# Mixer B's prompt attention with keys and values formed per head, mask and rotary rows in the contraction, and mixer A's units across both key groups

## The chip, the cores and the metric

The kernel runs on one core of one Trainium2 chip. The metric is the device time of one execution in microseconds, lower is better. All arithmetic is on 32-bit floats. The engines are TensorE (PE), which the profile splits into matmuls (PE) and weight loads (PEld), VectorE (DVE), ScalarE (ACT), GpSimd (POOL), and SyncE (SP), whose queue issues all DMAs here.

## The reference

Two layers of a streaming encoder run over 512 prompt tokens and, with the same weights, over 8 running streams of 16 new tokens each, so 640 tokens in all (T). Each layer has two attention mixers over one input projection, a gate, an output projection, and a gated feed-forward network. Mixer A is sliding-window attention (8 query heads in 2 key groups, head size 64). Mixer B is latent attention: keys and values are a shared latent of 128 numbers per token (ckv), and a rotary key of 32 numbers.

```python
    q = jnp.einsum('btr,rhe->bthe', _rms_norm(cq, q_norm), w_uq)      # 8 heads, 64 + 32 numbers
    q_rope = _rope(q[..., NOPE_DIM:], pos)
    q_lat = jnp.einsum('bthn,rhn->bthr', q[..., :NOPE_DIM], w_uk)
    ckv = _rms_norm(ckv, kv_norm)
    kr = _rope(kr, pos)
...
    s = (jnp.einsum('bqhr,bkr->bhqk', q_lat, ckv) + jnp.einsum('bqhe,bke->bhqk', q_rope, krope)).astype(f32) * MLA_SCALE
    if mask is not None:
        s = jnp.where(mask[None, None], s, -jnp.inf)
    p = jax.nn.softmax(s, axis=-1).astype(ckv.dtype)
    return jnp.einsum('bhqk,bkr->bqhr', p, ckv)
...
    y_b = jnp.einsum('bthr,rhv->bthv', o_lat, w_uv).reshape(B, T, HEADS_B * V_DIM)
    g = jax.nn.sigmoid(x @ w_gate + b_gate)
    h = g[..., :D_MODEL] * (y_a @ w_proj_a) + g[..., D_MODEL:] * (y_b @ w_proj_b)
    x = _layer_norm(ALPHA * x + h @ w_out, ln1_g, ln1_b)
```

The prompt's mask lets a query see all keys up to the end of its own chunk of 64 tokens. The score can be formed in two ways: the query is carried into the latent space (q_lat, 128 numbers) and meets ckv, or the latent is carried into each head's key space (64 numbers) and meets the query there. Likewise for the values and w_uv.

## The kernel before, in words

Features lie on partitions, tokens along the free axis. Weights come in slabs of 128 x 2048, through a ring of two buffers: SP loads w_raw, ACT rounds it to w_hi, POOL forms the rest w_lo, and PE multiplies three products of the high and low parts (`dense`). When POOL is done with a slab, its buffer is loaded anew (raw_free). The big products use a fast 32-bit form in one pass. The attention products are plain f32: one matmul in the program is two instructions in the trace, called passes here.

PE's work is a list of numbered jobs (J_ names), each written into one of four pairs of PSUM banks, with DVE or ACT emptying them; `start_job(n)` waits until job n-4 was emptied. A layer goes through these stages.

1. The input projection: cq, ckv, rotary key, the queries q_a of mixer A, k_t, v_t. Then NOPE and ROPE, the two parts of w_uq, then J_LAT (q_lat of each head, by `full` at L1244, from q_nope and a zero-padded w_uk called ukp), and J_TOK, transposes of v_t and ckv_t into tokens on partitions. DVE empties each: q_rs are copies of rotary queries of the streams (L940), v_tok, v_new, ckv_tok and ckv_new (L871) come last.
2. 40 attention units (UNITS). "Ap" is 128 prompt queries of mixer A (8 units, four heads of one key group each), "As" one stream of mixer A (8), "Bp" 128 prompt queries and two heads of mixer B (16), "Bs" one stream of mixer B (8). Bp and Bs units are mixed in the list. A Bp unit with block index i has (i+1) x 128 keys. A unit's steps are scores (PE), peaks (DVE), exps (ACT), normalise (DVE), turn (PE transposes the probabilities), a copy of one half on ACT and one on DVE, values (PE) and take_out (DVE). PE's order is written out by hand:

```python
                for u in range(NU):
                    turn(u)
                    gate_quarter(8 + 3 * u)
                    if u + 2 < NU:
                        scores(u + 2)
                    gate_quarter(9 + 3 * u)
                    values(u)
                    gate_quarter(10 + 3 * u)
```

A gate quarter is six matmuls of the gate's projection (L1438), so that PE has work while the other engines run a softmax. Four quarters fill one PSUM bank, which ACT copies to `logits` (take_gate, L696) before the next gate starts; SP stores the logits and loads the next gate slab, and also the cached rows of each Bs unit (load_cache).
3. J_UV: the latent outputs times w_uv (L1466 to L1468). ACT and DVE split y_a into ya_hi and ya_lo and the result into yb_hi and yb_lo, then PROJ multiplies them.
4. The output projection, norms, and the feed-forward network, which the change doesn't touch.

## Time and profile before

| | |
|---|---|
| median of 3 runs | 2150.72 us (2148.73 to 2151.97) |
| the profiled execution, its own time | 2150.01 us |
| its span, first to last instruction | 2148.2 us |
| mean granted TensorE clock | 0.973 of full |
| busy: PE, DVE, POOL, ACT | 94%, 46%, 31%, 31% of the span |
| issue to landing of a 1024 KB slab | 4.8 us |

A busy share says how much of the span an engine had work in flight. The granted clock is given as a share of 2.4 GHz; 0.5 is 1.2 GHz. A line such as L1438 is the line of the kernel before, the names behind it are the tile written and the tiles read.

### The profile page before, as it was taken

The numbers are of one execution on the slowest core, as the hardware profiler recorded it, in microseconds if no ns is written. First come the engines' busy times: TensorE is split into PE (matmuls) and PEld (weight loads), VectorE is DVE, ScalarE is ACT, GpSimd is POOL, SyncE is SP. The second block draws the span as 40 slices with busy tenths as digits, with TensorE's granted clock in tenths as the row PEclk, the third lists the DMA queues.
The fourth block names the chain that finished last, engine by engine and source line by source line (L and its number), as shares of the span: only waits on it lengthen the run. The fifth ranks groups of instructions, "written<-read, shape, count | busy, mean of one in ns | idle before, by whom it ended". The sixth has DMA issues, their size and how long they took to land.

```text
span 2148.2 us, 33773 instructions
## 1 busy us (share of the span) xinstructions
PE 2013.6 (94%) x12730; PEld 1856.9 (86%) x12730; DVE 984.2 (46%) x1437; ACT 656.7 (31%) x1303; POOL 675.3 (31%) x312
## 2 busy tenths in 40 slices
PE   6799999999899999999899899999998999999992
PEld 5786777789899999999899667777997999999992
DVE  3546433344765432443354753333476643234436
ACT  2213323242344311232231233223422542123222
POOL 2230111013823334333723111011262433343265
PEclk9899999999999999999999999999999999999996
DMA  5322121223112112211131212211421211222121
GB/s 143 115 97 78 50 97 61 74 82 128 59 54 83 68 70 83 82 62 62 69 136 55 95 58 78 78 57 50 157 79 40 91 66 60 81 95 78 49 72 70
DMA packets 49614, 169.86 MB, mean 79 GB/s; under 512 B 7128, under 2 KB 12024, under 8 KB 41272
## 3 DMA queue, kind: packets, MB, share of 16 engines
q1 hardware_dynamic: 49496, 168.28, 22.3%
q8 instruction: 76, 1.25, 0.2%
q14 instruction: 42, 0.34, 0.0%
HBM read 151.83 MB, written 18.26 MB: 79 GB/s over the span
## 4 chain that ended last, share of the span: by engine, by line
PE 74%; issue 13%; POOL 5%; DVE 5%; ACT 2%; DMA 1%; SPq 0%; POOLq 0%; DVEq 0%; ACTq 0%
PE ps L1236 50%; PE ps L1438 10%; POOL w_lo L546 4%; PE ps L1350 2%; PE ps L1347 2%; PE ps L1412 2%; PE ps L1370 1%; PE ps L1357 1%; PE ps L1244 1%; PE ps L1356 1%; POOL sum_sq L570 1%; ACT probs L663 1%; PE ps L1402 1%; PE ps L1416 1%; PE ps L1329 1%
## 5 line engine op out<-in xcount | busy, mean ns | idle before, releaser
L546 POOL TENSOR_TENSOR w_lo<-w_raw,w_hi 128x1024 fp32r<-128x1024 f32 (+3 forms) x252 | 577.1, 2299 | 1451.8 <-ACT w_hi L628 1440.9
L628 ACT ACTIVATE w_hi<-w_raw 128x1024 fp32r<-128x1024 f32 (+3 forms) x248 | 235.2, 968 | 486.2 <-PE ps L1236 466.7
L1236 PE MATMUL ps<-x_hi,w_hi 128*128 128x320 f32 x1504 | 345.7, 311 | 26.1 <-POOL w_lo L546 26.1
L1236 PE MATMUL ps<-x_lo,w_hi 128*128 128x320 f32 x1504 | 344.7, 310 | 0.0
L1236 PE MATMUL ps<-x_hi,w_lo 128*128 128x320 f32 x1504 | 344.2, 310 | 0.0
L1236 PEld LDWEIGHTS ps<-x_hi,w_hi 128*128 128x128 f32 x1504 | 253.0, 189 | 27.8 <-ACT w_hi L628 20.3
L1236 PEld LDWEIGHTS ps<-x_lo,w_hi 128*128 128x128 f32 x1504 | 253.2, 189 | 0.0
L1236 PEld LDWEIGHTS ps<-x_hi,w_lo 128*128 128x128 f32 x1504 | 253.2, 189 | 0.0
L1438 PE MATMUL ps<-x_hi,w_hi 128*128 128x320 f32 x512 | 184.9, 361 | 11.9 <-ACT logits L696 11.7
L1140 DVE TENSOR_SCALAR f_conv<-f_ext,vec 128x656 f32<-128x656 f32 x44 | 67.2, 1527 | 224.6 <-ACT tail L796 222.7
L1236 PE MATMUL ps<-hf_hi,w_hi 128*128 128x320 f32 x704 | 160.7, 309 | 0.0
L1236 PE MATMUL ps<-hf_lo,w_hi 128*128 128x320 f32 x704 | 160.4, 308 | 0.0
L1236 PE MATMUL ps<-hf_hi,w_lo 128*128 128x320 f32 x704 | 160.2, 308 | 0.0
L1438 PE MATMUL ps<-x_hi,w_lo 128*128 128x320 f32 x512 | 159.3, 311 | 0.0
L1438 PE MATMUL ps<-x_lo,w_hi 128*128 128x320 f32 x512 | 159.0, 311 | 0.0
L1438 PEld LDWEIGHTS ps<-x_hi,w_hi 128*128 128x128 f32 x512 | 97.2, 190 | 54.9 <-issue 36.5
L1236 PEld LDWEIGHTS ps<-hf_hi,w_hi 128*128 128x128 f32 x704 | 117.5, 188 | 0.3
L1236 PEld LDWEIGHTS ps<-hf_lo,w_hi 128*128 128x128 f32 x704 | 117.6, 188 | 0.0
L1236 PEld LDWEIGHTS ps<-hf_hi,w_lo 128*128 128x128 f32 x704 | 117.6, 188 | 0.0
L1155 DVE TENSOR_TENSOR hf_lo<-f_h,hf_hi 128x640 f32 x44 | 82.7, 1879 | 46.5 <-ACT hf_hi L804 46.5
L1263 PE MATMUL ps<-x_hi,w_hi 128*128 128x320 f32 x256 | 62.8, 329 | 38.5 <-DVE x_lo L1089 30.0
L1438 PEld LDWEIGHTS ps<-x_lo,w_hi 128*128 128x128 f32 x512 | 97.8, 191 | 0.7
(221 smaller groups left out, 3274.9 us busy)
## 6 DMA issues: line engine op xcount, KB each, us to landing
w_raw<-in_slabs SPq DMA_DIRECT2D x88, 1024.0 KB, 4.8
w_raw<-in_slabs SPq DMA_DIRECT2D x20, 768.0 KB, 4.2
gate_logits<-logits SPq DMA_DIRECT2D x32, 320.0 KB, 2.1
gates<-gate_logits SPq DMA_DIRECT2D x16, 640.0 KB, 6.1
w_raw<-in_slabs SPq DMA_DIRECT2D x16, 640.0 KB, 3.9
ckvc<-in_ckvc SPq DMA_DIRECT2D x16, 256.0 KB, 2.7
ckvc_t<-in_ckvc_t SPq DMA_DIRECT2D x16, 256.0 KB, 2.8
x_in<-in_x_t SPq DMA_DIRECT2D x4, 640.0 KB, 8.6
```

The lines of the kernel that those rows point to most:

```text
L546: pool.tensor_tensor(w_lo[:, s % 2, c], w_raw[:, s % 2, c], w_hi[:, s % 2, c].bitcast(F32), ALU.subtract).then_inc(wlo_ready, 1)
L570: pool.tensor_tensor(sum_sq[:], sq[:, 0, :] if k == 1 else sum_sq[:], sq[:, k % 2, :], ALU.add).then_inc(added_sq, 1)
L628: A(w_hi[:, s % 2, c], w_raw[:, s % 2, c], ACT.Copy).then_inc(whi_ready, 1)
L663: A(pr, pr, ACT.Exp, bias=st_nm[:, b, t:t + 1], accum_out=st_sum[:, b, t:t + 1])
L1140: link(TSC(f_conv[:, 0:NC_], f_ext[:, 2:EXT], w(2), vec[:, bass.ds(V_CB + j, 1)], ALU.mult, ALU.add))
L1155: TT(row(hf_lo, jj), f_h[:], row(hf_hi, jj).bitcast(F32), ALU.subtract).then_inc(fh_lo_ready, 1)
L1236: ins = MM(out_[:, a, :], w, x[:, t, a * HT:(a + 1) * HT], start=t == 0 and w is wh and x is hi, stop=t == tiles - 1 and w is wl)
L1263: ins = MM(out_[:, a, :], w, x[:, t, a * HT:(a + 1) * HT], start=t == 0 and w is wh and x is x_hi, stop=t == KD - 1 and w is wl)
L1347: MM(sc, q_lat[:, h, i * P:(i + 1) * P], ckv_t[:, 0:n], start=True, stop=False)
L1350: ins = MM(sc, q_r[hp, h // 4, i * P:(i + 1) * P], kr_r[hp, 0:n], start=False, stop=True)
L1412: ins = MM(o[:, 0:2 * P], ckv_tok[:, k, :], pt[:, k * 256:(k + 1) * 256], start=k == 0, stop=k == i)
L1438: ins = MM(ps[:, 7, 0:HT], w, x[:, t, a * HT:(a + 1) * HT], start=t == 0 and w is wh and x is x_hi, stop=t == KD - 1 and w is wl)
```

## The change

For the prompt's mixer B the latent is carried into each head's space once, before the units. `kb` holds for each head 64 key rows (w_uk times ckv, jobs J_KN, with w_uk turned by J_WUK first), 32 rotary key rows, and 4 mask rows; `qb` the same rows of the query. One contraction over 100 rows then gives the masked score. DMAs write the rotary rows and the mask rows. `v_b` holds values per head (jobs J_V), so a Bp unit's output is y_b itself and no longer the latent. J_LAT and J_UV remain for the streams alone. ckv_tok and the zero-padded ukp are gone. A Bp unit's values are now two column halves of 64 outputs, one for each head.

An Ap unit takes heads of both key groups, two of each, so that successive score matmuls use rows 0 to 63 and 64 to 127 in turn, and successive value matmuls write output partitions 0 to 63 and 64 to 127 in turn.

`logits` is half as large: each gate is stored by itself, and ACT waits for the store of the gate before the last. DVE waits for six of a layer's stores ahead of its first peaks, since tiles now share memory with what is stored.

```diff
-J_NOPE, J_ROPE, J_LAT, J_TOK = 13, 17, 21, 29
-J_UV = 33
-J_PROJ = J_UV + 4
+J_WUK, J_KN, J_NOPE, J_ROPE, J_LAT, J_V, J_TOK = 13, 14, 18, 22, 26, 27, 31
+J_UV = 34
+J_PROJ = J_UV + 1
...
@@ SyncE, before the layers and at a layer's start
+            sp.wait_ge(mask_made, 16)
+            sp.dma_start(bass.AP(mask_dram.tensor, 0, [[SEQ + P, NB], [1, CHUNK]]),
+                         inp["mask_q"][0:1, 0:CHUNK].broadcast_to([NB, CHUNK])).then_inc(mask_made, 16)
+            sp.dma_start(bass.AP(mask_dram.tensor, NB * SEQ + CHUNK, [[SEQ + P, NB], [1, CHUNK]]),
+                         inp["ones"][0:NB, 0:CHUNK]).then_inc(mask_made, 16)
+            sp.wait_ge(mask_made, 48)
...
+                sp.wait_ge(ckv_ready, layer + 1)
+                sp.wait_ge(kr_ready, layer + 1)
+                sp.dma_start(kb[NOPE + ROPE:KB, :, :], mask_dram[1].unsqueeze(1).broadcast_to([NB, HEADS, SEQ])
+                             ).then_inc(rows_loaded, 16)
+                sp.dma_start(kb[NOPE:NOPE + ROPE, :, :], kr_r[:, 0:SEQ].unsqueeze(1).broadcast_to([ROPE, HEADS, SEQ])
+                             ).then_inc(rows_loaded, 16)
+                for k in range(2):
+                    sp.wait_ge(qr_ready, layer * 2 + k + 1)
+                    for q in range(4):
+                        sp.dma_start(qb[NOPE:NOPE + ROPE, 4 * k + q, :], q_r[32 * q:32 * q + 32, k, 0:SEQ]
+                                     ).then_inc(rows_loaded, 16)
...
@@ ScalarE
-                for s in range(5, S_GATE + 2):
+                high(5)
+                high(6)
+                for k in range(4):
+                    job(J_KN + k)
+                    A(kb[0:NOPE, 2 * k, :], ps[0:NOPE, 2 * ((J_KN + k) % 4), :], ACT.Copy).then_inc(kn_even, 1)
+                for s in range(7, S_GATE + 2):
                     high(s)
+                for k in range(NB):
+                    job(J_V + k)
+                    A(v_b[:, k, :], ps[:, 2 * ((J_V + k) % 4), :], ACT.Copy).then_inc(v_b_ready, 1)
...
-                    if m >= 2 and g % 2 == 0:
-                        act.wait_ge(gate_stored[m % 2], layer * (16 * KD) + 16 * (m // 2))
+                    if m >= 1:
+                        act.wait_ge(gate_stored[g % 2], layer * (8 * NG) + 16 * m)
...
@@ VectorE, ahead of the first peaks
+                dve.wait_ge(stored, layer * (16 * N_STORE) + 16 * (N_STORE - 1))
...
@@ TensorE, ahead of the units
+                start_job(J_WUK)
+                for k in range(4):
+                    ins = pe.transpose(ps[:, 2 * (J_WUK % 4), k * P:(k + 1) * P], ukc[:, k, :], ident[:])
+                pe.wait_ge(job_taken, layer * NJ + J_WUK + 2)
+                for k in range(4):
+                    start_job(J_KN + k)
+                    MM(ps[:, 2 * ((J_KN + k) % 4), :], w_uk[:, k, :], ckv_t[:, 0:SEQ], start=True, stop=True
+                       ).then_inc(job_done, 1)
...
+                pe.wait_ge(job_taken, layer * NJ + J_LAT + 2)
+                for b in range(NB):
+                    start_job(J_V + b)
+                    MM(ps[:, 2 * ((J_V + b) % 4), :], ckv_t[:, b * P:(b + 1) * P], uv[:], start=True, stop=True
+                       ).then_inc(job_done, 1)
...
@@ TensorE, scores
-                        for t in range(GH):
-                            ins = MM(sc[:, t // 2, (t % 2) * WB:(t % 2) * WB + n], q_a[gp, t, i * P:(i + 1) * P],
-                                     k_t[gp, k0:k0 + n], start=True, stop=True)
+                        for t in range(2):
+                            for gg in range(GROUPS):
+                                gp = slice(gg * HD, (gg + 1) * HD)
+                                ins = MM(ps[:, bank + gg, t * WB:t * WB + n], q_a[gp, 2 * g + t, i * P:(i + 1) * P],
+                                         k_t[gp, k0:k0 + n], start=True, stop=True)
...
-                            MM(sc, q_lat[:, h, i * P:(i + 1) * P], ckv_t[:, 0:n], start=True, stop=False)
-                            MM(sc[:, n - CHUNK:], mask_q[:], ones[:, 0:CHUNK], start=False, stop=False)
-                            ins = MM(sc, q_r[hp, h // 4, i * P:(i + 1) * P], kr_r[hp, 0:n], start=False, stop=True)
+                            ins = MM(ps[:, bank + k, 0:n], qb[0:KB, h, i * P:(i + 1) * P], kb[0:KB, h, 0:n],
+                                     start=True, stop=True)
...
@@ TensorE, values
-                            ins = MM(o[:, 0:2 * P], ckv_tok[:, k, :], pt[:, k * 256:(k + 1) * 256],
-                                     start=k == 0, stop=k == i)
+                            for hh in range(2):
+                                h, hp = 2 * g + hh, slice(hh * VD, (hh + 1) * VD)
+                                c0 = k * 256 + hh * P
+                                ins = MM(o[hp, 0:P], v_b[:, k, h * VD:(h + 1) * VD], pt[:, c0:c0 + P],
+                                         start=k == 0, stop=k == i)
```

On TensorE, in the unit stretch of a layer, a step whose scores are those of a Bp unit with 512 keys reads as follows before the change. L1347, L1349 and L1350 are the latent, mask and rotary products, L1412 the values of another Bp unit, L1438 and L1519 the gate.

```order
L1347 MATMUL ps<-ckv_t,q_lat 128x512
L1349 MATMUL ps<-ones,mask_q 128x64
L1350 MATMUL ps<-kr_r,q_r 128x512
L1347 MATMUL ps<-ckv_t,q_lat 128x512
L1349 MATMUL ps<-ones,mask_q 128x64
L1350 MATMUL ps<-kr_r,q_r 128x512
...
L1438 MATMUL ps<-x_hi,w_hi 128x320
...
L1412 MATMUL ps<-probs_t,ckv_tok 128x256 x4
```

The same step after the change, on the same engine:

```order
L1519 MATMUL ps<-x_hi,w_lo 128x320
L1422 MATMUL ps<-kb,qb 128x512 x2
...
L1519 MATMUL ps<-x_hi,w_hi 128x320
L1519 MATMUL ps<-x_lo,w_hi 128x320
...
L1492 MATMUL ps<-probs_t,v_b 64x128 x8
```

Six matmuls of scores became two, and four value matmuls of 256 columns became eight of 128 columns and 64 outputs.

On TensorE, between the last job of the input projection (v_t) and NOPE, there is now this (before, NOPE followed at once):

```order
L1297 MATMUL ps<-x_hi,w_lo 128x320 x2
...
L1352 MATMUL ps<-ident,ukc 128x128 [waits par_loaded]
L1352 MATMUL ps<-ident,ukc 128x128 x3
L1354 REGISTER_ALU
L1355 REGISTER_ALU [waits ckv_ready]
L1271 REGISTER_ALU [waits job_taken]
L1358 MATMUL ps<-ckv_t,w_uk 128x512 [waits job_taken]
```

Four transposes, a wait for DVE's copy of them, and the first of four key products stand ahead of NOPE.

On SyncE, behind the second gate slab of a layer, after the change:

```order
L489 DMA kb<-mask_rows 4x8x512 [waits ckv_ready,kr_ready]
L491 DMA kb<-kr_r 32x8x512
L494 ISA
L497 DMA qb<-q_r 32x512 [waits qr_ready]
L497 DMA qb<-q_r 32x512 x3
L494 REGISTER_ALU
L497 DMA qb<-q_r 32x512 [waits qr_ready]
L497 DMA qb<-q_r 32x512 x3
L499 ISA
L501 DMA kc_t<-in_kc_t 128x1024 [waits job_taken]
```

Before, kc_t followed the second gate slab directly and waited for a job of J_LAT alone; ten DMAs and the waits for the rotary queries now stand ahead of it and of the stores behind it.

## Rows read from the trace of the kernel before

**Rows 1.** The page's first part: busy us, share of the span, instructions.

```profile
PE 2013.6 (94%) x12730; PEld 1856.9 (86%) x12730; DVE 984.2 (46%) x1437; ACT 656.7 (31%) x1303; POOL 675.3 (31%) x312
```

**Rows 2.** Busy time by stage of layer 0; last: clock, DMA share, GB/s.

```profile
core 0: us, PE busy (x) PEld busy (x) DVE busy (x) ACT busy (x) POOL busy (x), PEclk, DMA share, GB/s
145.00:163.00 18.00, 12.72 (x55) 8.66 (x53) 16.80 (x34) 1.57 (x2) 5.06 (x2) 0.91 0.52 171
163.00:180.00 17.00, 15.48 (x81) 14.16 (x82) 7.22 (x20) 6.82 (x23) 1.73 (x1) 0.80 0.29 118
180.00:236.00 56.00, 53.71 (x279) 37.33 (x277) 40.34 (x90) 22.36 (x76) 5.43 (x3) 1.00 0.09 32
273.00:458.00 185.00, 182.65 (x976) 141.28 (x976) 59.46 (x157) 53.04 (x129) 21.25 (x9) 1.00 0.18 62
```

**Rows 3.** Timeline of PE, scores of a Bp unit with 512 keys: start, us.

```profile
395.39 1.02 PE L1347 MATMUL ps<-ckv_t,q_lat 128*128 128x512 f32 x2
396.25 0.33 PE L1349 MATMUL ps<-ones,mask_q 128*128 128x64 f32 x2
396.51 1.12 PE L1350 MATMUL ps<-kr_r,q_r 32*128 32x512 f32 x2
397.56 1.12 PE L1347 MATMUL ps<-ckv_t,q_lat 128*128 128x512 f32 x2
...
399.83 0.41 PE L1438 MATMUL ps<-x_hi,w_hi 128*128 128x320 f32 x1
```

**Rows 4.** Timeline of PE: Ap scores, Ap values, Bp values.

```profile
209.30 1.99 PE L1329 MATMUL ps<-k_t,q_a 64*128 64x256 f32 x8
...
212.29 1.93 PE L1402 MATMUL ps<-probs_t,v_tok 128*64 128x512 f32 x4
...
454.67 1.89 PE L1412 MATMUL ps<-probs_t,ckv_tok 128*128 128x256 f32 x8
```

**Rows 5.** Timeline of PE, start of J_UV and two of its heads.

```profile
458.13 0.75 PE L1466 MATMUL ps<-q_lat,uv 128*64 128x320 f32 x2 [0.69 <-ACT logits L696]
...
458.73 0.48 PE L1466 MATMUL ps<-q_lat,uv 128*64 128x320 f32 x1
...
459.32 0.48 PE L1466 MATMUL ps<-q_lat,uv 128*64 128x320 f32 x1
```

**Rows 6.** Timeline of PE, first scores of a Bs unit.

```profile
273.15 1.12 PE L1356 MATMUL ps<-ckvc_t,q_lat 128*128 128x512 f32 x2 [0.16 <-DMA krc_t<-in_krc_t]
```

**Rows 7.** Timeline of DVE in the Ap units.

```profile
187.45 1.22 DVE L964 SCALAR_TENSOR_TENSOR probs<-ps,bias_p 128x1024 f32<-128x1024 f32 x1
...
194.02 1.22 DVE L964 SCALAR_TENSOR_TENSOR probs<-ps,bias_p 128x1024 f32<-128x1024 f32 x1
...
196.53 2.27 DVE L966 SCALAR_TENSOR_TENSOR st_nm<-st_mx,nsink_p 128x4 f32<-128x4 f32 x1
...
219.02 1.23 DVE L964 SCALAR_TENSOR_TENSOR probs<-ps,bias_p 128x1024 f32<-128x1024 f32 x1 [0.65 <-PE ps L1329]
```

**Rows 8.** Timeline of DVE and PE ahead of the units.

```profile
146.29 5.02 DVE L940 COPY q_rs<-q_r 32x128 f32<-32x128 f32 x4
...
152.22 6.26 PE L1244 MATMUL ps<-q_nope,ukp 128*128 128x320 f32 x16 [3.38 <-DVE q_lat L902]
...
158.76 1.04 PE L1312 MATMUL ps<-ident,v_t 128*16 128x128 f32 x8
...
163.06 0.48 PE L1329 MATMUL ps<-k_t,q_a 64*128 64x128 f32 x2 [1.95 <-DVE ckv_new L871]
```

**Rows 9.** Timeline of ACT at layer 0's start; DMA issues with us to landing.

```profile
61.80 1.15 ACT L628 ACTIVATE w_hi<-w_raw 128x512 fp32r<-128x512 f32 x2 [18.96 <-DMA w_raw<-in_slabs]
...
out_kc_keep<-in_kc_t SPq DMA_DIRECT2D x2, 448.0 KB, 6.3
...
bias_s<-bias_table SPq DMA_DIRECT2D x8, 9.0 KB, 1.6
```

**Rows 10.** Timeline of DVE and PE behind the units.

```profile
459.61 4.68 DVE L1035 TENSOR_TENSOR ya_lo<-y_a,ya_hi 128x640 fp32r<-128x640 f32 x4 [2.59 <-ACT ya_hi L721]
...
465.27 0.54 PE L1236 MATMUL ps<-ya_hi,w_hi 128*128 128x320 f32 x2 [1.68 <-DVE yb_lo L1038]
```

More of the change, by code:

```diff
@@ L120 @@
 NV = V_KVN + 1
[L124 removed]
+UNITS = [("Ap", i, g) for i in range(NB) for g in range(GH // 2)] + [("As", r, 0) for r in range(NREQ)]
 for _r in range(NREQ):
@@ L214, in build @@
         o += NB * P
-        v_new = place("v_new", o, [TDEC, NREQ, P])
-        ukp = place("ukp", o, [P, HEADS, KVL])
+        packed = place("packed", o, [P, NREQ * P])
+        v_new = packed[0:TDEC, :].rearrange("p (r n) -> p r n", r=NREQ)
+        q_rs = packed[ROPE:2 * ROPE, :].rearrange("p (r h n) -> p r h n", r=NREQ, h=HEADS)
+        ckv_new = packed[64:64 + TDEC, :].rearrange("p (r n) -> p r n", r=NREQ)
         o += NREQ * P
@@ L722, in _ @@
                 for k in range(4):
-                    job(J_UV + k)
-                    A(halves(yb_hi[:, k, :]), pair(J_UV + k), ACT.Copy).then_inc(yb_hi_ready, 1)
+                    act.wait_ge(job_taken, layer * NJ + J_UV + 2)
+                    A(yb_hi[:, k, :], y_b[:, k, :], ACT.Copy).then_inc(yb_hi_ready, 1)
                 def sigmoids(j):
@@ L928, in _ @@
                 take(J_VA, halves(v_t[:]))
+                take(J_WUK, w_uk[:].rearrange("p a n -> p (a n)"), ps[:, 2 * (J_WUK % 4), :])
                 for k in range(4):
-                    take(J_NOPE + k, halves(q_nope[:, k, :]))
+                    job(J_KN + k)
+                    dve.tensor_copy(kb[0:NOPE, 2 * k + 1, :], ps[NOPE:P, 2 * ((J_KN + k) % 4), :]).then_inc(kn_odd, 1)
+                    dve.wait_ge(kn_even, layer * 4 + k + 1)
+                    dve.wait_ge(kn_odd, layer * 4 + k + 1)
+                    dve.sem_inc(job_taken, 1)
+                for k in range(4):
+                    job(J_NOPE + k)
+                    src = pair(J_NOPE + k)
+                    for hh in range(2):
+                        hp = slice(hh * NOPE, (hh + 1) * NOPE)
+                        dve.tensor_copy(qb[0:NOPE, 2 * k + hh, 0:HT], src[hp, 0, :])
+                        dve.tensor_copy(qb[0:NOPE, 2 * k + hh, HT:SEQ], src[hp, 1, 0:SEQ - HT])
+                    dve.tensor_copy(q_nope[:, k, :], src[:, 1, SEQ - HT:]).then_inc(job_taken, 1)
                 for k in range(2):
@@ L1035, in _ @@
                     TT(ya_lo[:, k, :], y_a[:, k, :], ya_hi[:, k, :].bitcast(F32), ALU.subtract).then_inc(ya_lo_ready, 1)
+                take(J_UV, y_b[:, :, SEQ:], ps[:, 2 * (J_UV % 4), :].rearrange("p (k n) -> p k n", k=4))
                 for k in range(4):
                     dve.wait_ge(yb_hi_ready, layer * 4 + k + 1)
-                    TT(halves(yb_lo[:, k, :]), pair(J_UV + k), halves(yb_hi[:, k, :].bitcast(F32)), ALU.subtract
-                       ).then_inc(job_taken, 1)
+                    TT(yb_lo[:, k, :], y_b[:, k, :], yb_hi[:, k, :].bitcast(F32), ALU.subtract).then_inc(yb_lo_ready, 1)
                 for j in range(KD):
@@ L1353, in scores @@
                         pe.wait_ge(bs_loaded, layer * (48 * NREQ) + 48 * (i + 1))
-                        for to, lat, rot in ((ps[:, bank, 0:PAST], ckvc_t[:], krc_t[:]),
-                                             (ps[:, bank + 1, 0:TDEC], ckv_t[:, s0:s0 + TDEC], kr_r[0:ROPE, s0:s0 + TDEC])):
-                            MM(to, q_lat[:, i, SEQ:], lat, start=True, stop=False)
-                            ins = MM(to, q_rs[:, i, :, :].rearrange("p h n -> p (h n)"), rot, start=False, stop=True)
+                        old, new = ps[:, bank, 0:PAST], ps[:, bank + 1, 0:TDEC]
+                        rot = q_rs[:, i, :, :].rearrange("p h n -> p (h n)")
+                        MM(old, q_lat[:, i, :], ckvc_t[:], start=True, stop=False)
+                        MM(new, q_lat[:, i, :], ckv_t[:, s0:s0 + TDEC], start=True, stop=False)
+                        MM(old, rot, krc_t[ROPE:2 * ROPE, :], start=False, stop=True)
+                        ins = MM(new, rot, kr_r[:, s0:s0 + TDEC], start=False, stop=True)
                     ins.then_inc(scores_done, 1)
```

238 lines of the change are left out of this document (123 added, 115 removed).

## Prediction

> **What bounds the kernel now.** I read the page first [rows 1]: TensorE (PE) has work for 94% of the span, the next engine, VectorE (DVE), for 46%, so a change is worth what it takes off PE's queue, or what it adds to a wait of PE. The change touches only the attention part of each of the two layers, so I read that stretch by stage [rows 2]. In layer 0 it runs from 145 to 458 us. From 273 to 458 us (the units of mixer B) PE is busy 182.65 of 185 us at full clock, with DVE and ScalarE (ACT) busy for a third of it: a microsecond less on PE there is a microsecond less of time. From 180 to 236 us (mixer A's prompt units) PE is also nearly full, but DVE is busy 40 of 56 us, and its row of work is a second bound, see below. From 145 to 163 us PE has work for 12.7 of 18 us only: it waits for DVE. Layer 1 repeats these stages, so each sum counts twice. The records of one matmul overlap the next; I therefore price by the distance of starts, not by the durations.
>
> **Mixer B's prompt scores.** With 512 keys a unit now issues per head: latent pair (two passes, 0.86 us to the next start), mask pair (0.26), rotary pair (1.05), [rows 3]. The rotary pair has as many columns as the latent pair but costs 0.19 us more, since behind it the array goes from 32 rows back to 128: the weights of the next matmul aren't loaded under it. Both heads take 399.83 - 395.39 = 4.44 us, and the gate matmul behind them 0.10 more than its neighbours (0.41 against 0.31), so 4.54. Afterwards each head is one 128-column-wide contraction over 100 rows. No row shows one with 65 to 127 rows. Below, it costs what the 128-row latent pair costs (0.86; it can't be less, the columns are the same); above, it pays the 0.19 of a row change too. I take 0.86, as it is nearest in rows: 1.72 a unit, saved 2.82. Of that 1.71 is the rotary columns (2 x 0.855) and scales with the keys, 1.11 is fixed. Four units at each of 128, 256, 384 and 512 keys: 4 x (1.71 x 2.5 + 4 x 1.11) = 34.9 us a layer; with the row change on each head 32 x 0.19 = 6.1 less.
>
> **Its values.** A unit of 512 keys now issues 8 passes of 256 columns [rows 4]; by the 0.86 us of two passes of 512 a pass of 256 is 0.215, so 1.72. Afterwards 16 passes of 128 columns into two column halves of the array. That halves work side by side is seen in the old product with w_uv [rows 5]: a head has 640 columns in two passes each, which by 0.215 per 256 is 1.08 us, and the next head on the other half starts 0.59 us after it (458.73, 459.32). So I take the pairs as overlapped: 8 x 0.108. Against this stands a change of array shape on both sides, 0.19 on each side [rows 3], a little less for the narrower load, 0.36 in sum. Four units of each length: 4 x (10 x 0.215 - 4 x 0.36) = 2.9 us saved a layer. Without overlap it is 4 x 4 x 0.36 = 5.8 us lost.
>
> **Mixer B's streams.** A unit issues latent, rotary, latent, rotary products of 128 and 32 rows, with four changes of shape; the new order has two. 8 x 2 x 0.19 = 3.0 us a layer.
>
> **What eats into it.** A gate's last quarter must be copied out by ACT before the next gate may start; at the end of the stretch PE stood 0.69 us behind the tail (0.31) of its last matmul [rows 5], 1.0 from start to start where 0.15 is usual. What lies between, a turn, scores or values, hides it; scores of 128 keys shrink from some 2 us to 0.43, values to 0.58. With 20 gates in the stretch, a third ending before scores and a third before values, and the ACT a little later behind the exponentials (1.5 us), I put 2.3 us a layer. Second, the first stream unit has its cache load landing 0.16 us late now [rows 6]; that load is issued behind a gate slab that GpSimd frees, which doesn't come sooner, while PE comes some 1.5 us sooner (the first Bp scores): 1.5 us. Mixer B: 34.9 + 2.9 + 3.0 - 2.3 - 1.5 = 37.0 us a layer.
>
> **Mixer A's prompt units.** Scores of 8 passes last 1.99 us, values of 4 passes 1.93 us [rows 4]. In the new order neighbours lie on different row halves, or column halves, so each falls to about 1.1: 0.8 + 0.8 for the six units of 256 keys, half for two, 11 us of PE work a layer. But it isn't all on the path. DVE starts the bias step of units 3 and 4 at 187.45 and 194.02: 6.57 us for peaks, exponentials on ACT, normalising, peaks; in one round a small operation took 2.27 instead of 0.16 us while GpSimd ran [rows 7]. That loop stays as it is. From unit 4 on three rounds and one such meeting (2.1) bring unit 7's to 215.8, against 219.02 now, where it waits for PE. Behind it PE sets the pace, with three values 0.75 shorter each. 3.2 + 2.25, rounded down to 5 us a layer; none and 10 are the ends.
>
> **Ahead of the units.** PE gets four transposes (0.11 each by the row of eight, [rows 8]: 0.44), a wait for DVE to empty v and then w_uk (by 1.22 us for 1024 elements [rows 7] some 0.8 and 0.7, for 640 and 512; 1.4 us of it uncovered), and four f32 products of 512 columns, 4 x 0.86: 5.3 us in sum with nothing else for PE to do. Queued behind the key copies on ACT is the last part of the second w_uq slab (half 0 and 1); NOPE's 10.6 us on PE cover it. At the end most of the q_lat products go, but they were not the bound: the q_rs copies of DVE hold everything for 5.02 us beside GpSimd, PE waits 3.38 for them, and DVE's last copy ckv_new releases the first scores at 163.06 [rows 8]. The last ROPE product ends at 144.3, q_rs 7.0 later, the scores start 18.8 later. In the new chain behind the same q_rs copies come q_lat 1.4, four V products of 0.86 us, at half clock twice that, say 5.5, since PE has then idled 7 us; v_b and v_tok copies 1.5; v_new and ckv_new 2.4; with handovers about 18.3. So the start is 5.3 - 0.5 = 4.8 later, less 0.9 for the first two scores that overlap: 4 us lost a layer, 1 to 7 as ends.
>
> SP's queue: the kb rows, the eight qb rows, kc_t, vc and six stores now stand in a row behind the second qr_ready, 16 issues at about 0.5 us. PE waits for the rows; they land some 5 us before PE is there. DVE's peaks(0) now waits for the stores. The slowest lands 6.3 us after its issue [rows 9], the last at about 169 in layer 0's time; ACT takes up exponentials only after the first gate, at 175 then, so it costs nothing up to 2.7 us more.
>
> **Start of layer 0.** PE and ACT stand still for 19 us until slab 2 lands at 61.8, issued behind the parameters and bias_s [rows 9]. Two small mask copies, a wait for them (1.6 us as bias_s lands) and three more issues come in between: 2.4 us. In layer 1 PE is busy then: 0.4.
>
> **Behind the units.** The w_uv product shrinks from 5.3 us to about 1, but PE then waits for ya_lo, 4.68 us on DVE, and starts PROJ at 465.27 already because of DVE [rows 10]. yb_hi and yb_lo now come after ya_lo; PROJ's first 3.5 us cover most. Nothing gained; PE idles 5 us and may run at 1.2 GHz after it. 1 us lost a layer, 0 to 3.
>
> **Sum.** Per layer -37.0 - 5 + 4 + 1 = -37.0; two layers -74.0; start +2.8: -71.2 us. The profiled execution took 2150.01 (span 2148.2), the median is 2150.72; 2150 - 71 = **2079 us**.
>
> **Rivals.**
> (a) *Forecast*, 0.68, own range 2065 to 2096 by the ends of the small terms.
> (b) *The halves of the array don't share in the values.* Passes in series with exposed weight loads, half of the 0.1 us of a 128-wide one: 160 x 0.157 + 5.8 = 30.9 us in place of 14.4 a layer, and 3 in mixer A: +39, 2118. Against it the heads of [rows 5], 0.59 apart. 0.07. The Trainium skill says the like (TensorE: Matmul & The Clock Gate, "The mechanism" of Part 3): weight loads overlap a running matmul only where the row group differs, and these halves share all rows. By that rule 2118 would hold; the trace disagrees, since both heads of [rows 5] use all 128 rows.
> (c) *ACT and DVE become the bound of mixer B too*, through gates and exponentials; half its gain lost: 2116. For: PE's step at 128 keys falls to some 4 us. Against: both are a third busy [rows 2]. 0.06.
> (d) *The 100-row contraction pays the row change*, +12: 2091, with other small costs 2100. This is also the case that the change does less than it says. 0.04.
> (e) *More than forecast*: mixer A's loop shortens too and the new products hide; 2060. 0.12.
> (f) *Slower.* Shorter matmuls leave gaps in which the granted clock falls to 1.2 GHz in the unit stretch. It had 0.80 from 163 to 180 us [rows 2] behind idle times of 2 to 3 us. Some 255 us of a layer would be exposed; at half clock each microsecond costs one more, so it decides once 37 of them run so. With 45 of them 2079 + 90 = 2169. Against: the clock is 1.00 in every later stretch, and the work stays nearly gapless. 0.03.
>
> About 0.2% is what a measurement of this kernel can tell from no change. Faster 0.96, same 0.01, slower 0.03. The range 2062 to 2101 leaves out (b), (c), (f) and half of (e): two in ten.
>
> **What would show it.** One pair of passes per head, 0.86 us at 512 keys, and no mask or rotary rows; value pairs with starts together and 0.11 apart; the B stretch 37 us shorter at clock 1.00; DVE's round of 6.57 unchanged; first scores 4 to 5 us later; slab 2 at 64. I am wrong if value starts lie in series, if ACT logits release PE often, or if DVE stands before peaks(0) for stores.

## The result and the profile after

The changed kernel takes 2092.87 us (median of 4 runs, 2090.94 to 2094.47), the kernel before, on the same chip, 2150.81 us. The ratio is 0.9731, 95% interval 0.9714 to 0.9748. That is faster by 58 us, where I had forecast 71; 2092.87 lies in the range of 2062 to 2101. The profiled execution took 2092.84 us, its span 2090.9.

The page's first part, after (us busy, share of the span, instructions), answers to [rows 1]:

```profile
PE 1918.7 (92%) x12626; PEld 1803.5 (86%) x12626; DVE 977.6 (47%) x1429; ACT 665.1 (32%) x1319; POOL 675.5 (32%) x312
```

PE is busy 95 us less and the span only 57 us shorter, so some 38 us of it turned into idle time. To see where, I noted the time of the same events in both traces and took the differences stretch by stretch (after minus before, us; minus is a gain):

| stretch | forecast, each layer | layer 0 | layer 1 |
|---|---|---|---|
| start to the product of the input projection that waits 2.15 us for GpSimd (107.6 us before) | +2.4; layer 1 +0.4 | +3.8 | in the last line |
| to the first scores | +4.9 (4 with the 0.9 of the next line) | +5.5 | +5.2 |
| to the turn of unit 8 (Ap units) | -5.9 | -7.4 | -4.6 |
| to the first Bs scores (As units and the first Bp scores) | 0 (-1.5 for the Bp scores, +1.5 for the cache wait) | +0.6 | +0.6 |
| to J_UV (the other Bs and Bp units) | -37.0 | -34.9 | -34.9 |
| J_UV to the wait ahead of the FFN | +1 | +3.5 | +3.8 |
| from there to the next layer's same product, or the end | 0 | +1.7 | -0.3 |

The sum, before rounding, is -57.3. The lines with the two large misses are the fifth (2.1 us a layer) and the sixth (2.5 and 2.8). The fifth hides a larger loss, since its forecast also held 2.3 us for the gates' copies, which cost nothing there. PE's windows in layer 0 after (us, busy, granted clock, DMA share, GB/s) show what these places have in common, against [rows 2], where every stretch from 180 us on has 1.00:

```profile
162.00:172.40 10.40, 8.47 (x28) 0.74 0.81 252
...
182.30:208.10 25.80, 22.63 (x152) 1.00 0.17 61
208.10:212.60 4.50, 1.04 (x10) 0.90 0.00 0
212.60:220.00 7.40, 7.40 (x31) 0.60 0.06 22
220.00:273.00 53.00, 51.49 (x386) 1.00 0.19 66
275.70:288.00 12.30, 11.93 (x43) 0.58 0.19 62
288.00:424.70 136.70, 135.37 (x894) 1.00 0.23 78
432.20:436.60 4.40, 4.36 (x16) 0.50 1.04 410
```

Three stretches of PE work are at or near the 1.2 GHz level, each behind an idle time: 212.6 to 220, 275.7 to 288, 432.2 to 436.6. None of them is there in layer 0 before. Layer 1 has the same three and one more. In both layers PE waits 1.95 us for a gate's copy some 20 us into the Ap units; in layer 0 the clock stays up behind it, in layer 1 it falls (PE's rows and its windows):

```profile
192.44 0.42 PE L1519 MATMUL ps<-x_hi,w_hi 128*128 128x320 f32 x1 [1.95 <-ACT logits L740]
1204.76 0.45 PE L1519 MATMUL ps<-x_hi,w_hi 128*128 128x320 f32 x1 [1.95 <-ACT logits L740]
```

```profile
192.40:198.00 5.60, 5.56 (x38) 1.00 0.09 31
1204.70:1210.00 5.30, 5.24 (x26) 0.68 0.09 32
```

From the first scores to the first Bs scores layer 1 takes 106.2 us and layer 0 103.3, so this is where the 7.4 and 4.6 of the third line part. The runs below have one pattern or the other in either layer, which moves a profiled total by some 3 us. The kernel before has one slow stretch in the Ap units of its layer 1 as well, behind a gate wait of 1.92 us, but there it cost no time (110.2 us for the same part, 110.1 in layer 0):

```profile
1247.20:1257.00 9.80, 9.73 (x28) 0.65 0.00 0
```

The waits ahead of the three, after, from the timelines of PE, ACT, DVE and SP (start, us, then in brackets the idle time and what ended it); first the gate behind unit 4's turn, then the first Bs unit, then the tail:

```profile
212.04 0.51 ACT L740 ACTIVATE logits<-ps,vec 128x320 f32<-128x320 f32 x1
...
268.00 0.39 SPq L427 DMA_DIRECT2D w_raw<-in_slabs  x1
268.79 0.35 SPq L524 DMA_DIRECT2D ckvc<-in_ckvc  x1
...
270.17 0.34 SPq L526 DMA_DIRECT2D krc_t<-in_krc_t  x1
...
275.69 1.22 PE L1429 MATMUL ps<-ckvc_t,q_lat 128*128 128x512 f32 x2 [2.32 <-DMA krc_t<-in_krc_t]
...
426.49 2.60 ACT L765 ACTIVATE ya_hi<-y_a 128x640 fp32r<-128x640 f32 x4
427.24 4.66 DVE L1096 TENSOR_TENSOR ya_lo<-y_a,ya_hi 128x640 fp32r<-128x640 f32 x4 [2.90 <-ACT ya_hi L765]
432.24 0.87 PE L1297 MATMUL ps<-ya_hi,w_hi 128*128 128x320 f32 x2 [5.38 <-DVE ya_lo L1096]
```

At the cache, the gate slab's issue (268.00, when GpSimd has freed its buffer) stands ahead of the cache's in SP's queue, so nothing can land earlier. [rows 6] shows the same wait at 0.16 us. At the tail PE stood 1.68 us before [rows 10], since the old w_uv product kept it busy while DVE made ya_lo; now it stands 5.38.

The units themselves, from PE's timeline: scores of a Bp unit with 512 keys, up to the second gate matmul behind them, and its values:

```profile
390.81 1.88 PE L1422 MATMUL ps<-kb,qb 100*128 100x512 f32 x4
392.13 0.72 PE L1519 MATMUL ps<-x_hi,w_hi 128*128 128x320 f32 x1
392.68 0.32 PE L1519 MATMUL ps<-x_lo,w_hi 128*128 128x320 f32 x1
...
422.90 1.09 PE L1492 MATMUL ps<-probs_t,v_b 128*64 128x128 f32 x16
423.93 0.41 PE L1519 MATMUL ps<-x_hi,w_hi 128*128 128x320 f32 x1
```

Two heads of scores cost 392.68 - 390.81 - 0.15 (the gate matmul's own distance) = 1.72 us, exactly two 128-row pairs: 100 rows pay nothing. Sixteen value passes cost 1.03 us from start to start.

Ahead of the units (DVE and PE), against [rows 8]:

```profile
155.42 5.00 DVE L995 COPY packed<-q_r 32x128 f32<-32x128 f32 x4
160.45 1.29 DVE L1000 COPY q_lat<-ps 128x512 f32<-128x512 f32 x2
161.87 2.07 PE L1378 MATMUL ps<-uv,ckv_t 128*128 128x512 f32 x2 [7.12 <-DVE q_lat L1000]
```

The eight passes of V take 6.25 us to the next product. At layer 0's start SP's issues and ACT's first use of slab 2 (before, the first slab issue was at 55.20 and the copy at 61.80 [rows 9]):

```profile
48.87 0.65 SPq L406 DMA_DIRECT2D mask_rows<-in_mask_q  x1
49.56 0.56 SPq L408 DMA_DIRECT2D mask_rows<-in_ones  x1
51.95 0.39 SPq L462 DMA_DIRECT2D vec<-in_vec  x1
...
53.48 1.47 SPq L468 DMA_DIRECT2D ukc<-in_ukp  x2
...
55.53 1.34 SPq L474 DMA_DIRECT2D bias_p<-bias_table  x2
...
59.65 14.87 SPq L419 DMA_DIRECT2D w_raw<-in_slabs  x4
...
65.52 1.15 ACT L664 ACTIVATE w_hi<-w_raw 128x512 fp32r<-128x512 f32 x2 [22.37 <-DMA w_raw<-in_slabs]
```

### The profile page after: what moved, and what is told of

Its sections match the earlier page's. It is cut to its first block, busy times and chain, and to the rows that moved or that the text cites. A ratio compares the mean times of both kernels' runs of the same rounds, so it can differ in the third digit from the quotient of the medians.

```text
span 2090.9 us, 33733 instructions
## 1 busy us (share of the span) xinstructions
PE 1918.7 (92%) x12626; PEld 1803.5 (86%) x12626; DVE 977.6 (47%) x1429; ACT 665.1 (32%) x1319; POOL 675.5 (32%) x312
## 4 chain that ended last, share of the span: by engine, by line
PE 70%; issue 14%; POOL 6%; DVE 5%; ACT 2%; DMA 2%; SPq 0%; POOLq 0%; DVEq 0%; ACTq 0%
PE ps L1297 49%; PE ps L1519 11%; POOL w_lo L582 5%; PE ps L1422 2%; PE ps L1445 2%; DMA gates<-gate_logits 1%; PE ps L1492 1%; PE ps L1431 1%; POOL sum_sq L606 1%; ACT probs L707 1%; PE ps L1429 1%; PE ps L1496 1%; PE ps L1378 1%; DVE probs L1055 1%; ACT logits L740 1%
## 5 line engine op out<-in xcount | busy, mean ns | idle before, releaser
L1297 PE MATMUL ps<-x_hi,w_hi 128*128 128x320 f32 x1504 | 345.6, 311 | 29.8 <-POOL w_lo L582 29.8
L1297 PEld LDWEIGHTS ps<-x_hi,w_lo 128*128 128x128 f32 x1504 | 253.3, 189 | 0.0
L1519 PE MATMUL ps<-x_hi,w_hi 128*128 128x320 f32 x512 | 190.8, 373 | 19.0 <-ACT logits L740 18.8
L1519 PE MATMUL ps<-x_hi,w_lo 128*128 128x320 f32 x512 | 162.1, 317 | 0.0
L1519 PE MATMUL ps<-x_lo,w_hi 128*128 128x320 f32 x512 | 162.0, 316 | 0.0
L1519 PEld LDWEIGHTS ps<-x_hi,w_hi 128*128 128x128 f32 x512 | 99.4, 194 | 50.0 <-issue 24.5
L1519 PEld LDWEIGHTS ps<-x_lo,w_hi 128*128 128x128 f32 x512 | 100.5, 196 | 3.1 <-issue 1.9
L1519 PEld LDWEIGHTS ps<-x_hi,w_lo 128*128 128x128 f32 x512 | 99.9, 195 | 0.0
```

Of the source, the lines that this page charges most:

```text
L1297: ins = MM(out_[:, a, :], w, x[:, t, a * HT:(a + 1) * HT], start=t == 0 and w is wh and x is hi, stop=t == tiles - 1 and w is wl)
L1519: ins = MM(ps[:, 7, 0:HT], w, x[:, t, a * HT:(a + 1) * HT], start=t == 0 and w is wh and x is x_hi, stop=t == KD - 1 and w is wl)
```

## The experiments

My theory after these traces: each term of PE's work came about as forecast, and the 14 us went into waits that shorter work uncovers and, more than the waits themselves, into the slow clock behind them. The rivals: that the slow stretches have another cause, or that gains in one place are only waited for in the next. All runs are of the changed kernel with one edit unless said otherwise; 2092.9 is to be beaten. Ratios are to the kernel before on the same chip.

**The clock alone.** Three idle times are filled with products that nobody reads; no wait goes away.

```diff
+                def fill(to, n):
+                    for _ in range(n):
+                        MM(to, x_hi[:, 0, 0:P], x_hi[:, 0, 0:to.shape[1]], start=True, stop=True)
...
+                start_job(J_V)
+                fill(ps[:, 2 * (J_V % 4), 0:HT], 40)
                 pe.wait_ge(job_taken, layer * NJ + J_LAT + 2)
...
+                        if i == 0:
+                            fill(ps[:, bank, 0:HT], 16)
                         pe.wait_ge(bs_loaded, layer * (48 * NREQ) + 48 * (i + 1))
...
+                fill(ps[:, 7, 0:HT], 28)
                 for j in range(KD):
```

> TensorE gets throwaway products (fp32r, 128x128 by 320 columns, results overwritten) in three places where it stands idle in each layer of the changed kernel: 40 while it waits for the q_lat copy ahead of the V products (idle 7.39 us), 16 ahead of the first stream unit's scores (2.3 to 2.6 us), 28 behind the w_uv product ahead of PROJ (4.5 us). They fit into the idle time, so no wait goes away. Theory 1 (the missing gain is work done at the 1.2 GHz level after idle stretches): the granted clock stays at 1.00 behind these places; the V products take 3.4 instead of 6.25 us, the stretch from 277 to 287 us gives back 4.5, PROJ's first products 2.0; with a little for the transposes some 10 us a layer, 2073 us. Rival (the clock has nothing to do with it, the missing gain is in the waits or in contention): 2093 us, or a few us more for the added work.

Measured: 2071.39 us, ratio 0.9628 (0.9605 to 0.9652). PE's windows of this run behind the three places:

```profile
160.50:168.40 7.90, 5.88 (x28) 1.00 0.89 264
275.40:288.00 12.60, 11.85 (x83) 1.00 0.23 74
425.50:430.00 4.50, 3.82 (x25) 1.00 1.04 411
```

The V products take 3.54 us instead of 6.25 (2.7); from the first Bs scores to J_UV it is 145.9 and 146.1 us instead of 150.1 (4.1); from J_UV to the FFN's wait it is 125.2 us instead of 128.6 and 128.9, which is the 125.1 of before (3.5). Twice these three are 20.7 us. Adding work took 21 us off: the slow clock behind the waits costs this much, and the rival falls. In this profiled execution layer 0 was also 1.4 us quicker ahead of the fillers, since the clock stayed up behind the wait at 111 us; that part is chance, and layer 1 doesn't show it. The reader is to see that 275.4 to 288 has nearly twice as many matmuls (83 for 43) as the window above at nearly the same busy time.

**The cache load first.**

```diff
-                    for r in range(NREQ):
-                        if c == quarter_at_scores(AS_LAST if r == 0 else BS_UNIT[r - 1]):
+                    for r in range(1, NREQ):
+                        if c == quarter_at_scores(BS_UNIT[r - 1]):
                             load_cache(r)
                     if c % 4 == 3:
                         store_gate(c // 4)
+                    if c == 47:
+                        load_cache(0)
```

> The first stream unit's cache load is issued ahead of gate slab 6's load in SyncE's queue and no longer behind it. Theory 1 (the wait is queue order, and the slow clock behind it comes from the wait): the idle time of 2.3 us at 273 us goes, and with it the 1.2 GHz stretch from 277 to 287; 2 + 4.5 us a layer, 2080 us. Rival A (the wait goes, the clock falls anyway): -4 in all, 2089. Rival B (the gate slab behind it comes late instead, so the wait only moves): 2093.

Measured: 2078.71 us, 0.9667 (0.9643 to 0.9690). SP's issues, and PE's window behind the first Bs scores:

```profile
264.74 0.34 SPq L524 DMA_DIRECT2D ckvc<-in_ckvc  x1
...
268.03 0.38 SPq L427 DMA_DIRECT2D w_raw<-in_slabs  x1
```

```profile
273.00:285.00 12.00, 11.32 (x72) 1.00 0.21 64
```

The cache is issued 4.0 us sooner and the slab no later. From the first Bs scores to J_UV it is now 145.9 us against 184.98 before: 39.1 less. The three savings of the forecast come to 40.8 us, less 1.5 for the first Bp scores, which stand ahead of this stretch: 39.3. So the savings of mixer B were right, the 2.3 us for the gates' copies weren't lost here, and 4.2 us a layer were taken back by the clock alone. The fillers of e_fill, which leave the wait in place, bring the stretch to the same 145.9 us.

**Three V products ahead of the wait.** The wait for the q_lat copy is dropped on PE (the fourth product needs it for its bank and has it in `start_job`); DVE waits for its own copy before it counts V as taken.

```diff
-                pe.wait_ge(job_taken, layer * NJ + J_LAT + 2)
...
+                dve.wait_ge(job_taken, layer * NJ + J_LAT + 2)
                 for k in range(NB):
                     dve.wait_ge(v_b_ready, layer * NB + k + 1)
```

> TensorE no longer waits for the q_lat copy before the first of the four V products; only the fourth needs it (its bank). Theory (the wait is not needed, and V at 1.2 GHz is what it costs): three V products of 0.86 us at full clock lie under the 7.39 us of idle time, the first scores come some 4 us sooner a layer; 2085 us. Rival (DVE's copies of v_tok, v_new and ckv_new or the row loads set the scores' start anyway): under 1 us a layer, 2091 to 2093.

Measured: 2082.41 us (2077.78 to 2090.49), 0.9682 (0.9645 to 0.9718). PE now stands 4.28 us for the copy, behind three products instead of ahead of four, and the first scores start at 169.25 instead of 172.42 in layer 0, 3.2 us sooner where I expected 4. The runs spread by 13 us, so I read no more from them.

**PROJ row by row.**

```diff
-                    if j == 0:
-                        pe.wait_ge(ya_lo_ready, layer * 4 + 4)
-                    dense(J_PROJ + 2 * j, S_PROJ + k, half * KD, 4, ya_hi, ya_lo, half)
+                    dense(J_PROJ + 2 * j, S_PROJ + k, half * KD, 4, ya_hi, ya_lo, half,
+                          ready=(lambda t: pe.wait_ge(ya_lo_ready, layer * 4 + t + 1)) if j == 0 else None)
```

and the same for yb_lo.

> PROJ's first two jobs wait for ya_lo and yb_lo row by row instead of for all four rows. Theory 1 (TensorE's wait of 4.5 us for all of ya_lo and the slow clock behind it): PROJ starts 3.5 us sooner, DVE's rows of 1.17 us pace it, the clock stays nearer 1.00; 3 to 4 us a layer, 2085 us. Rival (the gain is given back waiting for yb_lo, whose last row ends at 436.3 us): 1 us a layer or less, 2091.

Measured: 2087.18 us, 0.9698 (0.9673 to 0.9722). From J_UV to the FFN's wait it is 124.5 and 124.9 us instead of 128.6 and 128.9: 4.1 and 4.0, the upper end. That is 8 us, but the median fell by 5.7 and the profiled execution by 4.5 only: in it the Ap units of layer 0 have the slow stretch that the changed kernel has in layer 1 alone, 3.0 us. PE's wait fell from 5.38 to 2.89 us; the first matmuls behind it are still 0.27 us apart (0.15 is usual), so part of the slow clock stays.

**The gate's copy first.** In `take_gate`'s place for the third quarter, ahead of `exps(u + 2)` for the units below 8.

```diff
+                    for g in range(NG):
+                        if gate_ends(g) == (u, 2) and u < 8:
+                            take_gate(g)
                     if u + 2 < NU:
                         exps(u + 2)
                     for g in range(NG):
-                        if gate_ends(g) == (u, 2):
+                        if gate_ends(g) == (u, 2) and u >= 8:
                             take_gate(g)
```

> ScalarE copies out a gate that ends in the third quarter of a unit ahead of the exponentials of two units later and no longer behind them (in mixer A's prompt units only). Theory (the 3.7 us idle behind the turn of unit 4 is the wait for gate 4's copy, which stands behind unit 5's exponentials, and it puts the next 6 us at 1.2 GHz): the idle time and the slow stretch at 212 to 218 us go, 4 to 6 us a layer, 2083. Rival (the DVE round of 6.57 us sets the pace, so the wait turns up at the values or the next turn): 1 us a layer or less, 2091 to 2093.

Measured: 2087.69 us, 0.9709 (0.9686 to 0.9732): 5.2 us, half of what I expected. The wait and the slow stretch at 212 us are gone (PE's window of 208 to 220 us):

```profile
208.00:220.00 12.00, 11.02 (x78) 1.00 0.17 69
```

but from the first scores to J_UV layer 0 gains only 0.8 us, layer 1 3.8. The two layers now take the same time, 252.5 us; layer 0 gains less because it has the slow stretch behind the 1.95 us wait, here 0.67 from 192.8 to 198, that the changed kernel has in layer 1 alone. Like with like, the edit gains 3.8 us a layer, short of 4 to 6. Part of the wait comes later, as the rival says, but with no slow clock behind it (1.00 from 221.7 to 234):

```profile
221.72 0.39 PE L1522 MATMUL ps<-x_hi,w_hi 128*128 128x320 f32 x1 [2.19 <-ACT logits L740]
```

**The mask copies early.** The two copies and the wait for them move ahead of `sp.wait_ge(table_stored, 16)`.

> The two mask copies and their wait stand ahead of SyncE's wait for the bias table's store, where SyncE is idle for 38 us, and no longer behind it. Theory (the later start of slab 2 is queue time on SyncE): 1.2 us for two issues and 2.0 us for the wait go, slab 2's first copy starts at 63.9 us instead of 67.1; 3 us in all, of which 2 to 3 reach the end: 2090 us. Rival (it's the traffic of the new row loads that delays slab 2): 67, 2093.

Measured: 2089.47 us, 0.9721 (0.9698 to 0.9745). The times in my expectation are those of PE's restart (67.6 after), which I had given to the copy; the copy on ACT comes 3.0 us sooner (65.52 above), as expected:

```profile
62.54 1.15 ACT L664 ACTIVATE w_hi<-w_raw 128x512 fp32r<-128x512 f32 x2 [19.82 <-DMA w_raw<-in_slabs]
```

**Do the halves of the array share?** Mixer B's values head by head:

```diff
-                        for k in range(i + 1):
-                            for hh in range(2):
+                        for hh in range(2):
+                            for k in range(i + 1):
```

> Mixer B's values of a unit are issued head by head (all key blocks of one head, then of the other), so neighbouring passes lie in the same column half of TensorE's array. Same work, same results. Theory (the column halves share the array, as in my sum): 16 passes of a 512-key unit take 1.72 instead of 1.02 us; 160 passes a layer, 7 to 9 us a layer more, 2107 to 2110 us. Rival (halves never shared, or neighbours in one half overlap as well): no change, 2093.

Measured: 2101.36 us, 0.9773 (0.9749 to 0.9797): 8.5 us lost, about half of the forecast. The values of a 512-key unit in this run, PE's timeline:

```profile
417.85 1.58 PE L1492 MATMUL ps<-probs_t,v_b 128*64 128x128 f32 x16
419.36 0.41 PE L1519 MATMUL ps<-x_hi,w_hi 128*128 128x320 f32 x1
```

1.51 us instead of 1.03; 384 keys 1.07 instead of 0.81; 256 and 128 keys unchanged. Four units of each make 3.0 us a layer, 6 of the 8.5; layer 1 lost this (2.9 from first scores to J_UV), layer 0 6.1, since it has the slow stretch in the Ap units too (0.94 from 183 to 210 us). Why sharing is only half lost is in the starts of the single passes:

```
417.85 418.01 418.12 418.23   one at a time
418.34 418.34 418.45 418.50 418.56 418.61 418.67 418.72   two abreast
418.83 418.94 419.05 419.16   one at a time
```

The trace doesn't name a pass's head; I read it from the spacing: there are two series of eight passes, each with 0.16 us to its second pass and 0.11 us from there on. So the second head's first pass starts together with the first head's fifth, ahead of its sixth.

**The same in mixer A:** group by group, scores and values.

```diff
-                        for t in range(2):
-                            for gg in range(GROUPS):
+                        for gg in range(GROUPS):
+                            for t in range(2):
```

and `k` and `gg` exchanged in the values.

> Mixer A's prompt units keep their two heads of both key groups, but scores and values are issued group by group, so neighbouring passes lie in the same row half (scores) or column half (values). Theory 1 (PE work grows by 0.85 us for scores and as much for values of a 256-key unit, but the DVE and ACT round of 6.57 us hides part): 12 us a layer of PE work, 3 to 6 us a layer of time, 2099 to 2105. Rival A (PE sets the pace): 2117. Rival B (the round hides it all): 2093.

Measured: 2094.18 us, 0.9745 (0.9721 to 0.9768): no change that can be measured. It looks like rival B, but not for its reason, since a unit's scores take no longer (184.09 to 185.16, as 184.25 to 185.31 in the changed kernel; [rows 4] has 209.30 to 211.22):

```profile
184.09 1.14 PE L1406 MATMUL ps<-k_t,q_a 64*128 64x256 f32 x8
185.16 0.42 PE L1519 MATMUL ps<-x_hi,w_hi 128*128 128x320 f32 x1
```

With four passes in each half, the second half's four start beside the first's in either order. So this run says nothing about how much the DVE round hides: it took no overlap away.

**Was the kernel before open to the same edits?** The kernel before, with the cache load and the gate copy moved in the same way.

> The kernel before with two of the orders tried above: the first stream unit's cache load ahead of gate slab 6's, and ScalarE's gate copy ahead of the exponentials in mixer A's prompt units. Theory (these waits are what the change uncovered, so the kernel before loses little by them): it had 0.16 us of wait at the cache and 2.2 us at the gate, with the clock at 1.00 behind both; 0 to 2.5 us a layer, 2146 to 2150 us. Rival (both orders help any kernel of this shape as they helped the changed one, 14 and 5 us): 2131.

Measured: 2146.49 us (2139.84 to 2151.06), 0.9979 (0.9966 to 0.9992): some 4 us in the medians, where the two edits gave the changed kernel 14 and 5. So the longer work before hid most of these orders, but not all: from the first scores to the first Bs scores the profiled execution, one of the slowest of the ten, gains 2.5 us in layer 0 and 5.7 in layer 1. Layer 1 loses 5.6 again behind the first Bs scores, where the clock falls although PE never stands for more than 0.4 us (PE's window):

```profile
1316.00:1328.00 12.00, 11.62 (x42) 0.50 0.12 44
```

Why it falls there is open. Measured between kernels that both have these orders, the change would be worth about 2146.5 - (2092.9 - 14.2 - 5.2) = 73 us, an estimate that adds two separate gains.

**All together.** The five edits and fillers for what idle time is left (30 products ahead of the fourth V product, 12 ahead of PROJ):

> The changed kernel with the five edits of the runs before together (cache load first, three V products ahead of the wait, PROJ row by row, gate copy first, mask copies early) and throwaway products for the 4.9 us of idle time left ahead of the fourth V product (30) and 2 us ahead of PROJ (12). Theory (the gains are of different places and add up: 14 + 10 + 6 + 5 + 3, with some 4 for the clock ahead of the first units): 2050 to 2056 us. Rival (waits behind one another: what is gained in one place is waited for in the next): 2065 or more.

Measured: 2046.51 us, 0.9519 (0.9503 to 0.9535), 3.5 us below the forecast's lower end. The five single gains come to 39 us, which would be 2053.9; the other 7 I put down to the fillers and to fewer slow stretches, which wasn't tried apart.

**The start.** The idle time at 45 us, 19.20 us before and 22.60 after, is a wait for slab 2, whose issue stands behind the bias table's store of 38 us. Loads that read the table move behind slab 4's:

```diff
-            sp.wait_ge(table_stored, 16)
...
                 for s in range(2, S_GATE):
                     load_slab(s)
+                    if s == 4:
+                        sp.wait_ge(table_stored, 16)
...
```

> As best_a, and the bias table's 38 us store no longer stands ahead of the first layer's parameters and slab 2 in SyncE's queue: the loads that read the table come behind slab 4's load, the mask of bias_p on DVE behind w_uk's copy. Theory (TensorE's 22 us of idle time at 45 us is a wait for slab 2 behind that store): the idle time goes and with it the 20 us at 1.2 GHz around it, of which TensorE works in some 12; best_a's time less 22 to 28 us, 2024 to 2032. Rival (the table's store takes the queues from slab 2's transfer too): less 5 to 10.

Measured: 2041.17 us, 0.9495 (0.9480 to 0.9511): 5 us less than best_a, the rival's figure; in the profiled executions it is 10, but best_a's was the slowest of its four. The idle time fell from 20.35 to 9.97 us. What is left, I took for a queue filled by the store (SP's issues took 4 to 5 us each), so ScalarE's queue issues it in the last run:

> As best_b, but ScalarE's queue issues the bias table's store, so that SyncE's issues no longer share a queue with it. In best_b the mask, vec, cos, sin and ukc issues took 4 to 5 us each on SyncE between 16 and 44 us where 0.4 is usual, and slab 2 was issued at 47.7 us. Theory (what is left of the wait is SyncE's issues held back by the full queue of the table's store): the issues take 0.4 us, slab 2 is in place before TensorE is through with its first jobs at 44.7, the 10 us of idle time there go and the slow stretch behind them; 10 to 14 us less than best_b's 2041, 2027 to 2031. Rival (the store fills the engines that all queues share): 2041.

Measured: 2036.84 us, 0.9466 (0.9449 to 0.9483), between theory and rival. SP's issues at the start of this run:

```profile
20.90 0.68 SPq L398 DMA_DIRECT2D mask_rows<-in_mask_q  x1
21.62 4.31 SPq L400 DMA_DIRECT2D mask_rows<-in_ones  x1
26.47 3.79 SPq L453 DMA_DIRECT2D vec<-in_vec  x1
30.32 4.98 SPq L454 DMA_DIRECT2D cos_t<-in_cos  x1
35.35 2.94 SPq L455 DMA_DIRECT2D sin_t<-in_sin  x1
```

All but the first are slow still, although the store is in another queue, so the full queue was not the cause; the store still ends sooner, since it is issued at 5.04 us instead of 6.59, and the idle time fell to 5.77 us. Why an issue takes 4 to 5 us beside this store stays open; running the slabs' issues ahead of the store altogether wasn't tried.

## Why the prediction was right, and where it was wrong

- **Scores, values and streams of mixer B: right.** 1.72 us for two heads of 512 keys over 100 rows, as the nearest row said; 16 value passes 1.03 us where my sum has 0.86 + 0.36 = 1.22, but the old ones took 1.54 from start to start instead of 1.72, so the saving of 0.5 stands. The stretch from the first Bs scores is 39.1 us shorter once no wait stands ahead of it (e_cache), for 39.3 by these savings. Rivals (b), (c) and (d) are out.
- **The term "first Bs cache load, 1.5 us" was the step that failed.** The wait was sized nearly right (2.32 instead of 0.16 us of idle time, 2.2 for 1.5), but I put nothing on the clock behind it: PE works the next 10 us at the 1.2 GHz level, 4.2 us a layer. I had the mechanism in rival (f), and asked there only whether it would turn the sign, not what it costs in places that I knew to wait.
- **"PE idles 5 us and may run at 1.2 GHz after it. 1 us lost, 0 to 3."** The idle time is 5.38 us and the clock fell. The tail costs 3.5 and 3.8, beyond my end: PE starts 0.7 sooner, then loses 2.2 at the slow clock (432.2 to 437; 5.76 us from the first ya to the first yb product, 3.60 before) and, 51 us on, 1.7 and 2.0 in a wait that wasn't there before, for DVE, which waits for the gates. Both went with the slow stretch in e_fill. That the second is caused by the first wasn't tried by itself.
- **Ahead of the units: right in kind, 0.6 and 0.3 too small.** V took 6.25 us instead of 5.5. The clock was in this sum, which is why it is close.
- **Start of layer 0: 1.4 too small.** The wait for the mask rows was some 2 us instead of 1.6, and the double ukc and bias_p issues took 1.47 and 1.34 us where I had three issues of 0.3.
- **Mixer A: the DVE round of 6.57 us stood** (bias steps at 193.21 and 199.78), and the 5.9 forecast lie between 7.4 and 4.6. That they lie between is partly luck: the two layers differ by a slow stretch behind the same wait of 1.95 us. Both would have gained more without the 4.50 us from turn 4 to the next gate matmul and the slow clock behind it. My "2.3 us a layer" for ACT's gate copies stood in mixer B, where PE is busy for 135.4 of 136.7 us (288 to 424.7); the wait came here. This term was put in the wrong place, and in the sum it covers part of the clock's cost in mixer B.
- **The DVE's wait for the stores: 1.75 us at 173.95, and it cost nothing,** since ACT took up exponentials only after the first gate, as forecast.

In sum, the 14 us that were missing are 4.2 in the Bs and Bp units (2 x 2.1: the clock took 4.2 a layer, and the 2.3 kept for the gates' copies weren't needed), 1.2 in the longer cache wait (2 x 0.6), 5.3 in the tail (2.5 + 2.8), 1.4 at the start, 0.9 ahead of the units and 1.0 between the layers and at the end (left open); the Ap units come out even.

The clock fell behind the waits of 2.3 to 5.4 us above, on a DMA, ACT and DVE alike. The Trainium skill (TensorE: Matmul & The Clock Gate, "HAM oscillation" in Part 1) tells of a wait for a transfer behind which every burst of matmuls starts slow. The traces agree for these three waits, but not for every shorter one: the clock stayed at 1.00 behind the 1.95 us in layer 0 and the 2.19 us in e_gate.

## What to carry to other kernels

Price a new wait on TensorE as the wait plus what the engine does behind it at half clock: here 2.3 us of waiting at the cache cost 6 to 7. Take it as the upper end for short waits, since behind some of 1.9 to 2.2 us the clock stayed up, and compare single layers and not only totals, since the same wait can fall out either way. When work on the bounding engine shrinks, go through the orders on the queues that feed it (which issue stands ahead of which, which copy ahead of which exponential), since most of their cost was hidden by the work that goes; three moves of this kind (e_cache, e_gate, e_mask) gave back 14.2, 5.2 and 3.4 us, more than the prediction had missed. Where an idle time cannot be removed, products that nobody reads are worth trying.

## What the runs showed that I had not expected

- **Halves of the array overlap over a distance.** Passes for the other column half need not alternate with those of the first: in e_serialb the second head's first pass starts with the first head's fifth, four passes ahead of its turn, and in e_seriala two blocks of four lose nothing. Only blocks of more than four passes do (0.48 us for eight and eight). The same page of the Trainium skill ("The mechanism" in Part 3) has matmuls start and end strictly in order, and weight loads overlap only across row groups. Here the pass of the second head starts ahead of the first head's sixth (418.34, 418.45), both heads on all 128 rows; the measurement decides.
- **More work, less time:** 84 added products a layer made the kernel 21 us faster.
- **Beside a store of 38 us the issues on another engine's queue take long:** 2.9 to 5.0 us each for four of the five shown above from best_c. Behind the store, in the changed kernel, vec, cos and sin take 0.4 us each.
- **The clock can fall without a wait in sight,** as in layer 1 of before_cg, where it cost 5.6 us.
